# Paired score bursts, a later turn back, and branch sums on GpSimd in two attention stages

## The reference, cut to what matters

```python
o_cmp = einsum(masked_softmax(q @ k_cmp - slope * dist_c), v_cmp)
o_slc = einsum(masked_softmax(q @ k_sel - slope * dist_s), v_sel)
o_win = einsum(masked_softmax(q @ k_win - slope * dist_w), v_win)
return g[0] * o_cmp + g[1] * o_slc + g[2] * o_win
```

## Time and profile before

| | |
|---|---|
| profiled execution | 2757.42 us, its span 2755.6 us, granted clock 0.999 |
| PE busy | 2711.6 us (98%) |
| DVE, ACT, POOL busy | 1440.7 us (52%), 1058.5 us (38%), 36.4 us (1%) |
| chain that ended last | PE 91%, DVE 4%, ACT 3%, issue 1%, POOL 1% |
| stretch 255 to 310 us | PE 50.45, DVE 32.28, ACT 31.80, POOL 21.07 us busy of 55 |

### The profile page before, as it was taken

The page is one execution under the profiler, slowest core; times in us unless marked ns, Lnnn a source line. Parts: engine busy times, 40 slices in busy tenths (PEclk is TensorE's granted clock), DMA queues, the critical chain, the costliest instruction groups (busy, mean ns, idle before and its releaser), DMA issues.

```text
span 2755.6 us, 38503 instructions
## 1 busy us (share of the span) xinstructions
PE 2711.6 (98%) x16358; PEld 2248.7 (82%) x16358; DVE 1440.7 (52%) x2360; ACT 1058.5 (38%) x1604; POOL 36.4 (1%) x62
## 2 busy tenths in 40 slices
PE   9988999999999999999999999999999999999998
PEld 7787788888887788888888888877888788888887
DVE  6834576643625756756346443274634544654433
ACT  5534454332425654433234222245433422432221
POOL 0000200000000000000000000001000000000000
PEclk9999999999999999999999999999999999999999
DMA  4200122222531002322323332236222232223222
GB/s 161 90 4 3 53 87 98 100 94 98 158 104 39 1 1 100 100 97 95 100 77 107 99 99 93 100 116 129 82 81 87 71 100 98 87 99 99 93 99 69
DMA packets 68686, 238.85 MB, mean 87 GB/s; under 512 B 7800, under 2 KB 10360, under 8 KB 68004
## 3 DMA queue, kind: packets, MB, share of 16 engines
q1 hardware_dynamic: 62256, 220.80, 23.9%
q10 hardware_dynamic: 6260, 15.59, 2.5%
HBM read 228.23 MB, written 6.03 MB: 85 GB/s over the span
## 4 chain that ended last, share of the span: by engine, by line
PE 91%; DVE 4%; ACT 3%; issue 1%; POOL 1%; DMA 0%; ACTq 0%; another core or an unknown queue 0%; DVEq 0%; POOLq 0%
PE psum L155 23%; PE psum L157 23%; PE psum L156 23%; PE psum L1330 3%; PE psum L1297 2%; PE psum L1317 2%; PE psum L843 2%; PE psum L201 2%; PE psum L202 1%; PE psum L209 1%; PE psum L1851 1%; PE psum L177 1%; PE psum L178 1%; PE psum L176 1%; PE psum L1987 1%
## 5 line engine op out<-in xcount | busy, mean ns | idle before, releaser
L155 PE MATMUL psum<-x_hi,w_hi 128*128 128x512 f32 x2128 | 846.1, 398 | 0.7 <-DVE w_lo L130 0.7
L157 PE MATMUL psum<-x_hi,w_lo 128*128 128x512 f32 x2128 | 830.4, 390 | 0.0
L156 PE MATMUL psum<-x_lo,w_hi 128*128 128x512 f32 x2128 | 829.5, 390 | 0.0
L130 DVE TENSOR_TENSOR w_lo<-raw,w_hi 128x1024 fp32r<-128x1024 f32 x409 | 500.2, 1225 | 391.7 <-ACT w_hi L123 391.6
L123 ACT ACTIVATE w_hi<-raw 128x1024 fp32r<-128x1024 f32 x409 | 427.9, 1050 | 306.0 <-DMA raw<-w_down 83.9
L155 PEld LDWEIGHTS psum<-x_hi,w_hi 128*128 128x128 f32 x2128 | 400.0, 188 | 90.6 <-issue 5.7
L156 PEld LDWEIGHTS psum<-x_lo,w_hi 128*128 128x128 f32 x2128 | 400.2, 188 | 85.5 <-issue 5.0
L157 PEld LDWEIGHTS psum<-x_hi,w_lo 128*128 128x128 f32 x2128 | 399.8, 188 | 83.8
L157 PE MATMUL psum<-h_hi,w_lo 128*128 128x512 f32 x616 | 240.0, 390 | 0.0
L156 PE MATMUL psum<-h_lo,w_hi 128*128 128x512 f32 x616 | 240.0, 390 | 0.0
L155 PE MATMUL psum<-h_hi,w_hi 128*128 128x512 f32 x616 | 240.0, 390 | 0.0
(11 more groups left out here) (412 smaller groups left out, 3298.5 us busy)
## 6 DMA issues: line engine op xcount, KB each, us to landing
raw<-w_up SPq DMA_DIRECT2D x88, 512.0 KB, 3.3
raw<-w_down SPq DMA_DIRECT2D x44, 512.0 KB, 3.3
raw<-w_f1up SPq DMA_DIRECT2D x44, 512.0 KB, 3.3
raw<-w_f2up SPq DMA_DIRECT2D x44, 512.0 KB, 3.3
raw<-w_qkv SPq DMA_DIRECT2D x36, 512.0 KB, 3.3
raw<-w_blend SPq DMA_DIRECT2D x28, 512.0 KB, 3.3
raw<-w_f1down SPq DMA_DIRECT2D x22, 512.0 KB, 3.3
raw<-w_f2down SPq DMA_DIRECT2D x22, 512.0 KB, 3.2
```

Source lines behind the costliest of these rows:

```text
L130: dve.tensor_tensor(self.w_lo[u % SLOTS][:], self.raw[u % SLOTS][:], self.w_hi[u % SLOTS][:].bitcast(F32), ALU.subtract).then_inc(self.lo_ ...
L155: pe.matmul(bank[:], hi, x_hi[:, kk], start=kk == 0, stop=False)
L156: pe.matmul(bank[:], hi, x_lo[:, kk], start=False, stop=False)
L157: mm = pe.matmul(bank[:], lo, x_hi[:, kk], start=False, stop=kk == kt - 1)
```

## The change

1. Scores, `mins`, `exps` and sink shifts of two parts are issued together in every even iteration, in place of one part in every iteration.
2. A finished tile is turned back four iterations behind its last part, not two (`BEHIND`), on PE, ACT and DVE; the order of `turn_bank` follows. The loops run to N + 4, and the early head takes two steps in each of the iterations N to N + 3.
3. In `nsa` the `tensor_reduce` on DVE goes. Two GpSimd additions of 128x128 (`add_branches`) take its place. `prod` becomes two buffers, and DVE waits for `taken` of two groups before. PE's wait for a free `out_bank` is for the product (`own`), not for the sum (`taken`).

```diff
+BEHIND = 4
-        done = p - 2
+        done = p - BEHIND
@@ mixes
-                pe.wait_ge(taken, g0 + g + 1 - len(out_bank))
+                if steps == 3:
+                    pe.wait_ge(own, o0 + steps * (g + 1 - len(out_bank)))
+                else:
+                    pe.wait_ge(taken, g0 + g + 1 - len(out_bank))
@@ PE
-        for p in range(N + 2):
-            if p + 2 < N:
-                scores(pe, p + 2)
+        for p in range(N + BEHIND):
+            if p % 2 == 0:
+                for q in range(p + 2, min(p + 4, N)):
+                    scores(pe, q)
...
-            back_to_features(p - 2)
-            if p >= N - 1:
+            back_to_features(p - BEHIND)
+            if p >= N - 4 + BEHIND:
                 head.pe(pe, 2)
@@ GpSimd
+    def add_branches(pool, p):
+        g = parts[p].group
+        prod, ob = mem.prod[g % 2], mem.ob[g % 8]
+        pool.wait_ge(own, o0 + steps * g + 3)
+        pool.tensor_tensor(ob[:], prod[:, 0:P], prod[:, P:2 * P], ALU.add).then_inc(paired, 1)
+        pool.wait_ge(paired, g + 1)
+        pool.tensor_tensor(ob[:], ob[:], prod[:, 2 * P:3 * P], ALU.add).then_inc(taken, 1)
...
-            if p + 2 < N:
-                shift_sinks(pool, p + 2)
+            if p % 2 == 0:
+                for q in range(p + 2, min(p + 4, N)):
+                    shift_sinks(pool, q)
@@ ACT
             if p < N:
                 copy(p)
-            features(p - 2)
-            if p + 2 < N:
-                exps(p + 2)
+            features(p - BEHIND)
+            if p % 2 == 0:
+                for q in range(p + 2, min(p + 4, N)):
+                    exps(q)
@@ DVE
-                dve.tensor_tensor(mem.prod[:]..., view[:, :, 0:HD],
+                if g >= 2:
+                    dve.wait_ge(taken, g0 + g - 1)
+                dve.tensor_tensor(mem.prod[g % 2][:]..., view[:, :, 0:HD],
                                   coef.unsqueeze(2).to_broadcast([P, n, HD]), ALU.mult).then_inc(own, 1)
-                dve.wait_ge(own, at + 3)
-                dve.tensor_reduce(mem.ob[g % 8][:]..., AX.X, ALU.add).then_inc(taken, 1)
...
-            if p + 2 < N:
-                mins(dve, p + 2)
+            if p % 2 == 0:
+                for q in range(p + 2, min(p + 4, N)):
+                    mins(dve, q)
...
-            lower(p - 2)
+            lower(p - BEHIND)
```

More of the change, by code:

```diff
@@ L1250, in paired_attention @@
             final_slot[key] = (p, n)
-        done = p - 2
+        done = p - BEHIND
         if done >= 0 and parts[done].last and groups[parts[done].group].t == TT - 1:
             order.append(("tile", groups[parts[done].group].tile))
-    for done in range(max(N - 2, 0), N):
+    for done in range(max(N - BEHIND, 0), N):
         if parts[done].last and groups[parts[done].group].t == TT - 1:
@@ L1261, in paired_attention @@
     m0, g0 = k.span("pa_mixed", N), k.span("pa_taken", G)
+    paired = sem("pa_paired")
     b0, h0, w0 = (k.span(f"pa_{n}", G // TT) for n in ("back", "high", "lowered"))
@@ L1363, in shift_sinks @@
         pool.tensor_tensor(mem.es[:, i:i + 2], mem.mn[:, i:i + 2], groups[parts[p].group].sinks, ALU.subtract).then_inc(shifted, 1)
+    def add_branches(pool, p):
[5 more added lines that the diff above has]
+        pool.tensor_tensor(ob[:], ob[:], prod[:, 2 * P:3 * P], ALU.add).then_inc(taken, 1)
     def pool(pool):
         if not sinks:
+            for p in range(N):
+                if parts[p].last:
+                    add_branches(pool, p)
             return
@@ L1454, in settle @@
             else:
-                dve.tensor_tensor(mem.prod[:].rearrange("p (s v) -> p s v", v=HD), view[:, :, 0:HD],
+                if g >= 2:
+                    dve.wait_ge(taken, g0 + g - 1)
+                dve.tensor_tensor(mem.prod[g % 2][:].rearrange("p (s v) -> p s v", v=HD), view[:, :, 0:HD],
                                   coef.unsqueeze(2).to_broadcast([P, n, HD]), ALU.mult).then_inc(own, 1)
-                dve.wait_ge(own, at + 3)
-                dve.tensor_reduce(mem.ob[g % 8][:].rearrange("p (h v) -> p h v", h=2),
-                                  mem.prod[:].rearrange("p (s h v) -> p h v s", h=2, v=HD), AX.X, ALU.add).then_inc(taken, 1)
         def lower(p):
@@ L2219, in attention_buffers @@
     mem.sm = [sb(f"{name}_sm{j}", [P, 16], stack=stack) for j in range(2)]
-    mem.prod = sb(f"{name}_prod", [P, 6 * HD], stack=stack)
+    mem.prod = [sb(f"{name}_prod{j}", [P, 6 * HD], stack=stack) for j in range(2 if name == "nsa" else 0)]
 def shape_constants():
```

## The result

The changed kernel takes **2763.03 us** (median of 12 runs, 2756.96 to 2767.53); the kernel before took 2757.8 us beside it (12 runs, 2755.92 to 2759.06). The ratio is 1.0019, interval [1.001, 1.0028]: 5.2 us slower, where 0.5 us faster was forecast. The spread is new: it was 3.1 us and is 10.6 us.

The account below looks back on a forecast made before the run. PE was taken to bound the kernel (busy 183.06 of 185 us in the sparse stage). The terms -10.9 - 2.5 + 12.3 + 0.6 + 0 = -0.5 us took 2758.2 to 2757.7 us, range 2749 to 2765.

Parts of the forecast that it names:

- Edit 1: Paired scores: each joined burst saves 0.35 us of PE, 10.9 us off in nsa; 0.6 us of waiting added.
- Rival D: Pairing saves only 0.22 us a burst, 3.1 us less gain outside iterations 2 and 3: 2761; chance 0.05.
- B: ACT's pair chain, not PE, sets the pace; second bursts wait for exponentials, 6.4 us: 2765; chance 0.14.
- Edit 2: Turning back four behind in nsa: 2.5 us off, but a new wait of 1.75 us seven times, 12.3 us on.
- Rival A: The turn-back bank in nsa is free in time, so no new wait: some 2744.5; chance 0.18 with its halves.
- no order of ACT's list lets that copy pass two exponentials: Argument against Rival A: ACT's copy that frees the turn-back bank in nsa stays behind the exponentials of parts 4 and 5.
- Edit 3: Sums on GpSimd in nsa: two additions, estimated 0.46 us each; DVE loses a 0.59 us reduce; effect taken as nothing.
- Rival C: DVE and GpSimd hold each other up, 0.92 us a group, at most 5.7 us; 2761 at half; chance 0.03.
- The lock that the forecast allowed for: In nsa, DVE's gate multiplication could be held for one GpSimd addition at a time; Rival C's mechanism, charged nothing.
- the sum: -10.9 - 2.5 + 12.3 + 0.6 + 0 = -0.5 us on 2758.2, so 2757.7 us.
- I take 0: swa stage: joined bursts give -2.5 us, ACT's later steps up to +3.8 and +0.8; taken as 0, bounds -3 to +4.
- gain and loss sit in the same iterations: Reason given for taking the swa stage at 0, near the middle of its bounds of -3 to +4.

Follow-up runs that it names:

- e5: e1 with ACT's copy of the odd part put between the pair's exponentials in the step before a turn back: 2749.11 us.
- e4: Changed kernel with scores paired on PE alone; mins, exponentials and sink shifts go one part an iteration as before: 2801.43 us.
- e8: e1 with the branch sums back on DVE's reduction instead of GpSimd's additions: 2759.29 us.
- e1: Changed kernel with the window stage (swa) back in its old order, the sparse stage (nsa) as changed: 2759.59 us.
- e11: e5 with the branch sums back on DVE's reduction instead of GpSimd's additions: 2748.68 us.
- e2: Changed kernel with the sparse stage (nsa) back in its old order and sums, the window stage (swa) as changed: 2758.49 us.
- e6: e1 with seven matmuls that nobody reads before each of seven turn backs in the sparse stage: 2755.72 us.
- e9: Changed kernel with unread matmuls at both idle places, eighteen in the tail of swa and seven before each of seven turn backs: 2757.52 us.
- e10: Changed kernel with one edit: before a turn back in nsa, ACT's copy of the odd part goes between the pair's exponentials: 2752.33 us.
- e3: Changed kernel with eighteen matmuls that nobody reads in the tail of swa: 2764.82 us.

## Why the prediction was wrong

**Edit 1, right in size.** A joined burst is worth the 0.35 us that was read from the earlier trace rows: iterations 0 and 1, and 4 and 5, came within 0.03 us of the forecast, 6 and 7 within 0.06. Rival D is out. B's waits were nearly absent (5.73 us against 5.79; 1.7 us in 3 times on score bursts over the whole stage); they come in e5, where ACT does the second part later, and in full in e4.

**Edit 2, right in mechanism and nearly in size.** The new wait is 1.54 us, not 1.75, seven times, on the line and for the reason given. Rival A needed the copy ahead of the second part's exponentials: "no order of ACT's list lets that copy pass two exponentials" was true of the list as written and false of a list with one line moved, which is e5 at 2749.11.

**Edit 3, right.** Two additions of 0.45 us (estimate 0.46), no effect on the time that shows in two pairs of kernels (0.3 us from e8 to e1, 0.4 from e11 to e5, both within the spread). Rival C is out. The lock that the forecast allowed for between the gate multiplication and a GpSimd addition was not put to the test: the gate multiplication took 0.17 us before and after, and in the profile none of the 32 ran beside one of the 64 additions.

**The step that failed is the sum.** It has only durations at one clock and no term for what a stretch of idle PE does to TensorE's clock afterwards. The durations came out: by the profiles the sparse stage took 1.0 us less and the window stage 1.1 more (e2), together +0.1, against -0.5 forecast. The missing term is at two places. The `swa` stage, at which the forecast says "I take 0" (bounds -3 to +4): measured +5.0 in the profiled execution, of which 1.1 are the edits (e2's profile) and 3.9 the spell at 1.2 GHz. The bounds counted ACT's guest steps and copies, but not DVE's queue: the settle that frees the only output bank went behind two parts' minimums, and "gain and loss sit in the same iterations" passed over the tail, where nothing is left to gain. And the turn back's 12.3 us were priced as a wait alone; filling that wait with useless work gives back 3.9 us (e6 against e1), and filling both places 4.7 of the 5.2 (e9 and the changed kernel, each against the kernel before beside it). That e9's 2757.52 is within 0.2 us of the forecast is in part luck, since it holds the fillers' own time. How the loss of a usual execution divides between the two places is not shown. The profile before gave no warning by itself, since its clock is 1.00 in the whole stage; but the forecast had put a wait of some 1.75 us into a cycle where the longest idle time written on a weight load was 0.76.

It is luck too that 2763.03 lies in the stated range of 2749 to 2765: the range reached that far up for rival B, whose waits did not come.

The Trainium skill tells of something near this, in "TensorE: Matmul & The Clock Gate", section "A second HAM failure mode: psum-queue depth-cycling": a PE that often idles briefly between groups of matmuls can swing between its two clock levels and lose throughput. This case agrees that short idle times can come ahead of a fall, but here they are single waits, 1.16 us once in `swa` and 1.54 us once in a cycle of 21.33 us.

**Open.** Why a wait of 1.16 or 1.18 us came ahead of a fall in the changed kernel and in e10, and not in e2's profile, the runs don't settle. The same page of the Trainium skill, Part 1, section "What's actually happening", says that what judges PE's activity runs freely and does not start anew with a kernel, so that one kernel differs from run to run. This fits the spread, but no run here tests it. Nor does any profile show where an execution of the changed kernel at 0.994 loses its time: its profiled one lost it in `swa` alone, and e8, whose profile lost it at the turn backs, is another kernel.

## What to carry to other kernels

A wait that a change puts onto an otherwise dense TensorE costs its own length and, in some executions, a spell at half clock behind it: here 1.8 us (e1, two spells in 3.6) to 3.9 us for a wait of 1.2 to 1.5. When work is paired on an engine, look for what it used to let through between the two: a copy or a settle that frees the only buffer belongs between the halves of the pair. To tell a clock effect from a cost, fill the wait with work that nobody reads; if the time falls, it was the clock. If it doesn't, little is shown, for the filling can cost time itself (1.5 us in e3).

## What was not expected of the hardware

Added work made a kernel faster: 98 matmul records without use (seven matmuls in each of seven waits) took 3.9 us off (e6 against e1). The granted clock at the end of `swa` stayed at 0.50 for 8 us in which PE was busy throughout (302 to 310, 4.00 of 4.00 us in both stretches), so a spell is much longer than the wait ahead of it. And a mean clock lower by 0.001 to 0.005 over 2760 us was enough to hide a 0.2% change: the mean of a run is worth reading beside its time.
